# A two-block transformer kernel: the norm of y by Ln and Exp on ScalarE a pair later, and VectorE's takes and mixes ahead of its splits

## What is computed

```python
# ssd_branch: y from ssd_scan (32 heads, 8 groups, chunks of 128 tokens)
y = y + xs * d_skip[:, None]
# gated_group_rms_norm(y, z, w, groups=8)
g  = y * silu(z)
gs = g.reshape(..., 8, 256)
gs = gs * rsqrt(mean(square(gs), axis=-1) + 1e-6)
y_b = gs.reshape(g.shape) * w
# first_block
mixed = sigmoid(gate_a) * (y_a @ w_branch_gm) + sigmoid(gate_b) * (y_b @ w_branch_ssm)
x = x + g1 * (mixed @ w_out)
```

## Time and profile before

| what | value |
|---|---|
| median of 3 runs | 1638.83 us (1637.58 to 1642.01) |
| the profiled execution | 1638.96 us, span 1637.2 us |
| busy share of the span | PE 97%, VectorE (DVE) 61%, ScalarE (ACT) 47%, GpSimd (POOL) 10% |
| mean granted clock of TensorE | 0.982 of full speed |
| the scan | about 251 us to 397 us of the span |
| branch_ssm, then the stage out | 397 us to 444 us, 444 us to 472 us |
| DMA | 289.68 MB, 177 GB/s over the span |

### The profile page before, as it was taken

One profiled execution on the slowest core, in us unless ns is written; L12 is line 12 of the kernel. 1 busy time (PEld: TensorE's weight loads), 2 busy tenths in 40 slices (PEclk: granted clock), 3 DMA queues, 4 the chain that ended last, 5 costly groups with the idle time before them and its releaser, 6 DMA issues.

```text
span 1637.2 us, 30488 instructions
## 1 busy us (share of the span) xinstructions
PE 1588.5 (97%) x12680; PEld 1540.2 (94%) x12680; DVE 998.6 (61%) x1281; ACT 773.7 (47%) x1017; POOL 162.4 (10%) x132
## 2 busy tenths in 40 slices
PE   7999999988999999999999899999999999899997
PEld 5999998877999999999999789999999999899997
DVE  5876895344776645655466666554665557775545
ACT  3544555443455534544444455444544445554433
POOL 0100002333200001000012002000210013020001
PEclk9999999989999999999999999999999999999999
DMA  8974763222545555455545324555355554345550
GB/s 318 366 264 155 293 230 125 101 78 96 184 148 189 185 190 191 156 181 185 191 162 181 129 103 180 179 183 191 141 205 179 180 182 153 135 175 183 185 194 30
DMA packets 42154, 289.68 MB, mean 177 GB/s; under 512 B 4843, under 2 KB 7019, under 8 KB 7500
## 3 DMA queue, kind: packets, MB, share of 16 engines
q1 hardware_dynamic: 41244, 284.44, 47.8%
q0 software_dynamic: 816, 3.87, 0.6%
HBM read 285.15 MB, written 3.15 MB: 176 GB/s over the span
## 4 chain that ended last, share of the span: by engine, by line
PE 88%; DVE 6%; ACT 3%; issue 2%; DMA 1%; POOL 0%; SPq 0%; ACTq 0%; DVEq 0%; POOLq 0%
PE banks L612 21%; PE banks L615 21%; PE banks L614 21%; PE banks L713 6%; PE banks L715 6%; PE banks L716 6%; DVE w_lo L1599 2%; ACT w_hi L1160 1%; DVE XS L1747 1%; PE banks L958 0%; PE banks L744 0%; PE banks L869 0%; DMA raw<-in_panels 0%; PE banks L961 0%; DVE H L1755 0%
## 5 line engine op out<-in xcount | busy, mean ns | idle before, releaser
L1599 DVE TENSOR_TENSOR w_lo<-raw,w_hi 128x1024 fp32r<-128x1024 f32 x490 | 612.6, 1259 | 510.8 <-ACT w_hi L1160 505.5
L1160 ACT ACTIVATE w_hi<-raw 128x1024 fp32r<-128x1024 f32 x490 | 515.0, 1057 | 560.9 <-PE banks L615 408.3
L612 PE MATMUL banks<-H,w_lo 128*128 128x256 f32 x1920 | 541.8, 282 | 2.2 <-DVE H L1755 1.6
L614 PE MATMUL banks<-H,w_hi 128*128 128x256 f32 x1920 | 540.2, 281 | 0.0
L615 PE MATMUL banks<-H,w_hi 128*128 128x256 f32 x1920 | 540.2, 281 | 0.0
L612 PEld LDWEIGHTS banks<-H,w_lo 128*128 128x128 f32 x1920 | 361.3, 188 | 5.3 <-issue 3.4
L614 PEld LDWEIGHTS banks<-H,w_hi 128*128 128x128 f32 x1920 | 361.4, 188 | 0.0
L615 PEld LDWEIGHTS banks<-H,w_hi 128*128 128x128 f32 x1920 | 361.4, 188 | 0.0
L614 PE MATMUL banks<-HH,w_hi 128*128 128x256 f32 x960 | 270.1, 281 | 0.0
L612 PE MATMUL banks<-HH,w_lo 128*128 128x256 f32 x960 | 270.1, 281 | 0.0
L615 PE MATMUL banks<-HH,w_hi 128*128 128x256 f32 x960 | 270.1, 281 | 0.0
(11 more groups left out here) (285 smaller groups left out, 1716.9 us busy)
## 6 DMA issues: line engine op xcount, KB each, us to landing
raw<-in_panels SPq DMA_DIRECT2D x269, 1024.0 KB, 4.8
bias_rows<-rev POOLq DMA_DIRECT2D x1, 2048.0 KB, 16.9
XS<-in_x_t SPq DMA_DIRECT2D x1, 1024.0 KB, 6.5
near<-bias_rows POOLq DMA_DIRECT2D x8, 128.0 KB, 3.0
out_t<-XS SPq DMA_DIRECT2D x4, 256.0 KB, 2.6
ws<-in_ws_t POOLq DMA_DIRECT2D x1, 512.0 KB, 9.3
cols<-in_cols SPq DMA_DIRECT2D x1, 180.0 KB, 2.4
wdt<-in_wdt POOLq DMA_DIRECT2D x1, 128.0 KB, 5.7
```

What stands on the lines that cost most here:

```text
L612: pe.matmul(acc, w_lo[:, panel_slot, at:at + P], operand[:, kk, 0, :], start=starts and c == chunks[0], stop=False)
L614: pe.matmul(acc, w_hi[:, panel_slot, at:at + P], operand[:, kk, 1, :], start=False, stop=False)
L1160: act.activation(w_hi[:, sl, w], raw[:, r, w], ACT.Copy).then_inc(panel_hi, 1)
L1599: vec.tensor_tensor(w_lo[:, sl, w], raw[:, r, w], w_hi[:, sl, w], ALU.subtract).then_inc(panel_lo, 1)
```

## The change

It does six things.

1. `y_roots` takes Ln and then Exp with a scale of -0.5 in place of Sqrt, after a preload of the table set that has both, and the reciprocal in `y_normed` is gone.
2. For groups 0 to 3 `y_roots(0, 4)` stands behind the splits and the Tanh of pair 10, no longer ahead of them.
3. `y_normed`, `y_hi` and `y_lo` of groups 0 to 3 come a pair later each.
4. In pair 15 VectorE's `y_variance(6)` and `skip(14)` come ahead of the split and the two `gate_times`.
5. In the last two panels of branch_ssm VectorE makes both mixes first and then split, rest, split, rest; ScalarE makes both splits first and then rounds both mixes.
6. `y_variance` of groups 4 to 7 also waits until `y_normed` has read the slot of `st` that it writes.

```diff
@@ gpsimd
-                if 11 <= n < 15:
-                    y_lo(n - 11)
+                if n >= 12:
+                    y_lo(n - 12)
@@ scalar
             def y_roots(first, count):
                 act.wait_ge(S["y_var"], first + count)
                 at = first % 4
-                act.activation(st[:, at:at + count, :], st[:, at:at + count, :], ACT.Sqrt).then_inc(S["y_root"], count)
+                if first == 0:
+                    act.preload_act_table_set("natural_log_exp_and_others")
+                act.activation(st[:, at:at + count, :], st[:, at:at + count, :], ACT.Ln).then_inc(S["y_log"], count)
+                act.wait_ge(S["y_log"], first + count)
+                act.activation(st[:, at:at + count, :], st[:, at:at + count, :], ACT.Exp, scale=-0.5)\
+                    .then_inc(S["y_root"], count)
...
-                if n == 10:
-                    y_roots(0, 4)
                 if n >= 2:
                     y_square(n - 2)
                 for q, half in fill_halves(n):
...
-                if n == 11:
+                if n == 10:
+                    y_roots(0, 4)
+                if n == 12:
                     act.wait_ge(half_used, 2 * AT["gate_b", 1, 1] + 2)
-                if 11 <= n < 15:
-                    y_hi(n - 11)
+                if n >= 12:
+                    y_hi(n - 12)
...
                 for half in range(2):
                     split_half(q + SPLIT, half)
+                for half in range(2):
                     if p == 3:
@@ vector
             def y_variance(g):
                 vec.wait_ge(S["y_sums"], g + 1)
+                if g >= 4:
+                    vec.wait_ge(S["y_f"], 2 * (g - 3))
...
             def y_normed(g):
                 vec.wait_ge(S["y_root"], g + 1)
-                step(vec.reciprocal(st[:, g % 4, :], st[:, g % 4, :]))
...
+                if n == PAIRS - 1:
+                    y_variance(6)
+                    skip(n - 1)
                 for q, half in fill_halves(n):
                     split_half(q + SPLIT, half)
...
-                if 10 <= n < 14:
-                    y_normed(n - 10)
-            y_variance(6)
-            skip(PAIRS - 2)
+                if 11 <= n < 15:
+                    y_normed(n - 11)
             skip(PAIRS - 1)
...
                 for half in range(2):
-                    split_half(q + SPLIT, half)
                     if p == 3:
                         mixed(g, half)
+                    else:
+                        split_half(q + SPLIT, half)
                 if n < 4:
                     y_normed(4 + n)
                 if p == 3:
-                    mixed_rest(g, 0)
-                    mixed_rest(g, 1)
+                    for half in range(2):
+                        split_half(q + SPLIT, half)
+                        mixed_rest(g, half)
```

More of the change, by code:

```diff
@@ L295, in two_blocks @@
             "sgu_vn sgu_vt sgu_vcopy sgu_mix sgu_y sgu_hi sgu_lo ws_masked "
-            "wdt_hi wdt_lo dt_raw dt_y dt_exp dt_one dt_ln dt_ea dt_a cum_done cum_got cum_hi cum_lo "
+            "wdt_hi wdt_lo dt_raw dt_y dt_exp dt_one dt_ln dt_ea dt_a y_log cum_done cum_got cum_hi cum_lo "
             "cb_done cb_copied xt_done xdt_done row_done exp_done never_set m_done y_done y_skip "
```

## The result

The changed kernel takes 1623.78 us (median of 4 runs, 1620.36 to 1624.73), the kernel before beside it 1639.57 us (1637.58 to 1642.01, 4 runs). The ratio is 0.9899, with a 95% interval from 0.9879 to 0.9919: 15.8 us or 1.0% faster. The forecast was 1621.0, 18 us less than before.

What follows compares the result with a forecast made beforehand. TensorE, busy for 97% of the span, was taken as the bound, with only idle time and slow clock to win: idle 11.0 plus clock 7.0 made 18.0, from 1638.96 to 1621.0 us; range 1616 to 1629.5.

Steps and rivals of the forecast that it cites:

- the scan's part: From pair 9's `group_sums` to branch_ssm's first matmul: 68.2 us before, 50.0 without waits, 18.2 lost; 51 to 55 forecast.
- Sqrt behind the Tanh: Pair 10: TensorE's wait for gate_b's Tanh falls from 2.00 to about 0.3, gain 1.7; 0.9 stays ahead of `group_sums(4)`.
- Reciprocal gone: Pairs 12 to 14 of the scan: waits for `y_variance` fall, gain 3.1, and that of `group_sums(5)` to 0.6, gain 1.7.
- part 2: Scan, pairs 11 to 14: VectorE loses the 1.74 us reciprocal, 0.80 of `y_normed` remains; gains 3.1 and 1.7.
- the cover of about 1 us in pair 14: Pair 14: added `y_normed` costs nothing, `y_square(13)` being ready about 1 us before TensorE finishes its half; otherwise 0.8.
- Take ahead of the split: Pair 15: `head_outputs(15)` waited 2.74 for `skip(14)`; 0.7 left, gain 2.0.
- Groups 4 to 7 worth nothing: In branch_ssm VectorE's list is shorter by 4 x 1.74, but TensorE was never idle there: gain 0.
- Mixes: Last panels of branch_ssm: the second panel of `out` no longer waits 2.46 for MX, gain 2.5.
- The clock: Low clock lost 7.0 in the scan and 1.6 behind 452.71; 7.0 of 8.6 won back.
- the bracketed waits: TensorE's waits read from the scan's rows, together 11.2 us of the 18.2 lost; the other 7 were taken as slow clock.
- the fall of 1.6: One low-clock stretch worth 1.6 us assumed to stay, as waits of 0.9, 0.6 and 0.7 stand next to short matmuls.
- the end: From branch_ssm's first matmul to ff1's: 2.5 for the wait for MX and 1.6 of slow clock, 4.1 in all.

Runs made afterwards that it cites:

- fillers: The kernel before with never-read matmuls put in front of TensorE's six long scan waits and its wait for MX: 1630.62 us against 1639.15, ratio 0.9952.

## Why the prediction was right, point by point

The sign, the mechanism and, to within 2.2 us, the size held: 18.0 us forecast, 15.8 measured, inside the range. Two of the signs that the prediction asked for did not come: the scan's part took 57.1 us and not 51 to 55, and one wait for `y_variance` was over 0.5.

1. **Sqrt behind the Tanh.** Forecast: wait 0.3, then 0.9 ahead of `group_sums(4)`. Measured 0.21 and 0.83. Right, with Ln and Exp at the 1.06 that the nearest row gave. The Trainium skill (ScalarE: Activation LUTs, section "What ACT_TABLE_LOAD costs") states a drain of 1.38 us on top of each load that switches the set. The trace doesn't agree: Ln starts 1.30 us after the start of a load of 1.28, and the wait is 0.83 and not the 2.3 that a drain would have made.
2. **Reciprocal gone.** Pairs 12 and 13 about as forecast (0.31 and 0.59 for 0 and 0.6). Pairs 14 and 15 were mis-sized. The forecast left 0.2 for `y_variance(5)` and nothing ahead of `group_sums(6)`, with `y_normed` at 0.80; it took 1.88 and 1.91 beside GpSimd's `y_lo`, and the waits are 0.86 and 0.49. This is the step of part 2 that failed: the cost of `y_normed`, and with it the cover of about 1 us in pair 14. I had counted the split as stretched by GpSimd and not the multiplications. In the kernel before, the reciprocal stood between, and `y_lo` was over before they began.
3. **Take ahead of the split.** Forecast 0.7 left, measured 0.68.
4. **Groups 4 to 7 worth nothing.** Shown by the reciprocals put back there, which TensorE never waited for.
5. **Mixes.** Wait for MX gone; 4.6 us with the clock, forecast 4.1.
6. **The clock.** One low stretch of 3.4 us stayed, as taken. But the scan's low clock was worth 5.4 us (fillers; 5.8 with the wait that grew), not 7.0. I had taken it as the rest after the bracketed waits, and those read short by some 0.2 us each: the period from 326.72 to 343.96 is 1.45 longer than a clean one, its two waits say 1.04.

The terms of the miss: the scan gained 11.1 in place of 13.9 (15.5 less the fall of 1.6), the end 4.6 in place of 4.1. Most of the 2.8 are the 1.15 us of the two longer waits and the 1.6 of the clock.

## What to carry to other kernels

Price an instruction by where it stands: four reciprocals of one size were worth 7 us in front of what TensorE waited for and nothing among back-to-back panels. Where a short wait of TensorE is removed, count the low clock behind it too, and take that from the distance of equal work, not from what the bracketed waits leave over. Group ScalarE's functions so that the last user of the other table set is already past, and load the next set while ScalarE waits anyhow.

## What was not expected of the hardware

- VectorE's multiplication with two tensor inputs (128 x 256) took 0.48 us alone. One that began while GpSimd's `y_lo` ran took 1.49 and 1.52 us and ended 0.28 and 0.29 us after it. The reciprocal, with one tensor input, took its 1.74 us beside `y_lo` too. `y_lo` itself took 1.81 to 2.00 us where VectorE's split ran beside it, and about 1.28 elsewhere.
- Ln and Exp in turn, behind a Tanh and with no new preload, each had a table load of 1.28 us before it (six for three pairs).
- Which waits are followed by a stretch at 1.2 GHz differs between executions whose scan is the same. The changed kernel had its one stretch behind the wait of pair 14, both times; its copy with the reciprocals in branch_ssm had it behind that of pair 12. The kernel before had three, and its copy with only the mixes moved had four, two of them at waits that had none before. What decides it stays open, and so does why a wait of 2.46 for MX was followed by one in the kernel before and not in the kernel with the take alone.
